# One kernel on one core: the shift columns of the opening on TensorE, the loads of the opening in another order, and three waits of the pair loop moved

## The chip, the core and the metric

One NeuronCore of a Trainium2 chip runs the whole program. The metric is device time in microseconds (us), the median of several executions. Engines are called TensorE (PE in the rows, PEld its weight loads), VectorE (DVE), ScalarE (ACT), GpSimd (POOL) and SyncE (SP, which issues most DMAs).

## What is computed

Two blocks on x (512 tokens, 1024 features, fp32). The change touches the first one:

```python
mod = jax.nn.silu(c) @ w_ada[layer] + b_ada[layer]
shift, scale, gate = jnp.split(mod[:, None, :], 3, axis=-1)
h = rms_norm(x, norm_g[layer]) * (1.0 + scale) + shift
proj = h @ w_in[layer]           # hq hf hi hz rq rk rv rz ga gb
# oA: HGRN2 over chunks, 8 heads; oB: retention over chunks, 8 heads
uA = head_rms_norm(oA, hg_norm_g[layer]) * silu(hz)
uB = head_rms_norm(oB, ret_norm_g[layer]) * silu(rz)
m = sigmoid(ga) * uA + sigmoid(gb) * uB
x = x + gate * (m @ w_out[layer])
```

Retention's q and k are turned (rotary: the two halves of 32 rows of each head are swapped and combined with cos and sin). The second block (convolution, banded attention, two feed-forward layers) follows.

## The kernel before

Features lie on partitions: KC = 8 chunks of 128 features, T = 512 tokens along the free axis. An fp32 product is made of three faster ones: x is split into xa_hi and xa_lo, each weight chunk into w_hi and w_lo, and `dense` does, for each of 8 k, three matmuls of 512 columns (hi x hi, hi x lo, lo x hi): 24 matmuls a chunk (lines 1379 to 1381). A weight chunk of 512 KB is loaded by SyncE into one of four slots of w_raw, ScalarE makes w_hi (`w_high`, line 495), GpSimd makes w_lo (`w_low`, line 431); `ahead(I, j)` on ScalarE makes the w_high of three chunks later. Each engine works through its own program in order; semaphores join them.

**Opening.** x (two DMAs of 1 MB), the scale and shift columns of w_ada (`ada_w`, 8 DMAs of 1 MB: for chunk c the 128 scale columns and the 128 shift columns) and the first four weight chunks are loaded, interleaved. ScalarE squares x, TensorE sums the squares over partitions with a matrix of ones (`sum_squares`), ScalarE makes rstd. VectorE makes silu(c) on all partitions (`c_wide`) and, in `modulation(c)` (lines 908 to 914), two reductions of 1024 elements, one for the scale column and one for the shift column, and the gain column `mix_gain`. `scaled_input(c)` (923) is x * gain * rstd, ScalarE adds the shift column in place (548) and copies to xa_hi (549), GpSimd makes xa_lo for chunks 0 to 5 (438), VectorE for 6 and 7 (929). TensorE computes the first three weight chunks k by k as xa arrives, then chunk 3, and goes into `pair(0)`.

**Pair loop.** Four times (two heads of each kind): 20 weight chunks. The order on TensorE is written out by hand: chunks 0 to 3, `dense_tokens(4)` (values, 96 matmuls of 256 columns, lines 1408 to 1410), 6 and 7 (rotary q and k), `hgrn_levels(0)`, `dense_tokens(10)`, `hgrn_rest(0)`, 12, `ret_scores(0)`, `(1)`, 13, `ret_scores(2)`, `(3)`, `attend(0, 0)`, 14 and so on to 19. The forget gates come from chunks 0 and 1 (ScalarE's sigmoid, line 596, VectorE 1055 to 1059, ScalarE's Ln 603, VectorE's scans and exponents, ScalarE's Exp 567, VectorE's `decayed`, 982 to 996). After that ScalarE copies the values out (616), and for chunks 6 and 7 copies the PSUM bank to `rqk` (623) and, turned, in four pieces of 32 rows to `unit` (626); then comes `ahead(at(7 + n), ...)`, the w_high of chunks 10 and 11. VectorE masks the scores (`near_levels`, `near_eye` line 1018, `causal` 1028 to 1032) out of the four banks of `aps`; a bank is free again when its `taken` semaphore counts up, and TensorE's `attend` waits for that.

## Time and profile before

| | us |
|---|---|
| median of 3 runs | 1752.26 (1751.93 to 1752.62) |
| the profiled execution | 1750.22 |
| its span in the trace | 1748.4 |
| TensorE busy in it | 1671.2 |
| VectorE, ScalarE, GpSimd busy | 809.3, 766.7, 672.1 |

Times in the rows are us from the start of the span. A row of the timeline is: start, duration, engine, line and instruction, what it writes and reads, how many instructions are merged in it, and in brackets how long the engine had idled before it and what ended that. An instruction that waits for the memory port after it has started shows a longer duration.

### The profile page before, as it was taken

What the parts mean: (1) busy time and instruction counts of PE and PEld (TensorE: products, weight loads), DVE (VectorE), ACT (ScalarE), POOL (GpSimd) and SP (SyncE); (2) the same over time, 40 slices, a digit from 0 to 9 for tenths busy, and PEclk for the clock granted to TensorE, in tenths of its full rate; (3) what the DMA queues carried; (4) which work ended last, traced back from release to release, by engine and by line L of the source; (5) the groups of instructions that cost most, each with busy time, mean ns of one, the idle gap of its engine ahead of it and who ended that gap; (6) DMA issues with size and microseconds to landing.
All of it is one profiled execution on the core that took longest, in us unless ns stands there. A gap on an engine that the chain in (4) does not pass through costs nothing.

```text
span 1748.4 us, 22097 instructions
## 1 busy us (share of the span) xinstructions
PE 1671.2 (96%) x8005; PEld 1360.0 (78%) x8005; DVE 809.3 (46%) x1391; ACT 766.7 (44%) x1179; POOL 672.1 (38%) x281
## 2 busy tenths in 40 slices
PE   4899999999999999998999999999999999999997
PEld 2777877877877778875888888888887888888885
DVE  6864564564565539994322122126465321121123
ACT  4544554553553664646443222226476442222222
POOL 3343343343343434312444444445223444344342
PEclk7999999999999999998999999999999999999999
DMA  9321331331331446201223223223211333222231
GB/s 373 103 91 57 103 105 60 101 102 50 107 98 58 134 70 183 96 1 44 90 95 103 89 96 101 92 96 120 73 49 60 98 96 96 96 96 96 96 96 61
DMA packets 49876, 167.59 MB, mean 96 GB/s; under 512 B 4987, under 2 KB 9500, under 8 KB 49308
## 3 DMA queue, kind: packets, MB, share of 16 engines
q1 hardware_dynamic: 43696, 154.50, 26.6%
q10 hardware_dynamic: 6124, 12.33, 3.0%
q8 instruction: 38, 0.62, 0.2%
q14 instruction: 18, 0.15, 0.0%
HBM read 161.56 MB, written 5.24 MB: 95 GB/s over the span
## 4 chain that ended last, share of the span: by engine, by line
PE 83%; DVE 8%; ACT 4%; issue 3%; POOL 1%; DMA 0%; ACTq 0%; DVEq 0%; POOLq 0%
PE gps L1379 23%; PE gps L1381 23%; PE gps L1380 22%; POOL w_lo L431 1%; DVE ada_w L910 1%; PE gps L1408 1%; PE gps L1630 1%; PE gps L1632 1%; PE gps L1631 1%; PE gps L1409 1%; PE gps L1410 1%; PE aps L1548 1%; PE aps L1682 1%; DVE at_near L1005 1%; DVE gates L1125 1%
## 5 line engine op out<-in xcount | busy, mean ns | idle before, releaser
L431 POOL TENSOR_TENSOR w_lo<-w_raw,w_hi 128x1024 fp32r<-128x1024 f32 x260 | 644.8, 2483 | 980.6 <-ACT w_hi L495 980.6
L1379 PE MATMUL gps<-xa_hi,w_hi 128*128 128x512 f32 x1152 | 460.3, 400 | 21.2 <-POOL xa_lo L438 13.3
L1381 PE MATMUL gps<-xa_hi,w_lo 128*128 128x512 f32 x1152 | 450.5, 391 | 0.0
L1380 PE MATMUL gps<-xa_lo,w_hi 128*128 128x512 f32 x1152 | 450.3, 391 | 0.0
L495 ACT CAST w_hi<-w_raw 128x1024 fp32r<-128x1024 f32 x260 | 270.9, 1045 | 154.4 <-PE gps L1381 137.0
L1379 PE MATMUL gps<-xb_hi,w_hi 128*128 128x512 f32 x736 | 291.6, 396 | 2.4 <-issue 1.2
L1381 PE MATMUL gps<-xb_hi,w_lo 128*128 128x512 f32 x736 | 288.9, 393 | 0.0
L1380 PE MATMUL gps<-xb_lo,w_hi 128*128 128x512 f32 x736 | 286.3, 389 | 0.0
L1379 PEld LDWEIGHTS gps<-xa_hi,w_hi 128*128 128x128 f32 x1152 | 217.5, 189 | 74.9 <-issue 18.5
L1380 PEld LDWEIGHTS gps<-xa_lo,w_hi 128*128 128x128 f32 x1152 | 217.7, 189 | 46.2 <-issue 3.1
L1381 PEld LDWEIGHTS gps<-xa_hi,w_lo 128*128 128x128 f32 x1152 | 217.3, 189 | 46.0
L1379 PEld LDWEIGHTS gps<-xb_hi,w_hi 128*128 128x128 f32 x736 | 138.4, 188 | 33.0 <-issue 3.6
L1381 PEld LDWEIGHTS gps<-xb_hi,w_lo 128*128 128x128 f32 x736 | 138.2, 188 | 32.0
L1380 PEld LDWEIGHTS gps<-xb_lo,w_hi 128*128 128x128 f32 x736 | 138.2, 188 | 31.1 <-issue 0.5
L1284 DVE TENSOR_TENSOR hbuf<-gps,rstd 128x512 f32<-128x512 f32 x44 | 30.4, 692 | 202.1 <-PE gps L1381 202.1
L1227 DVE SCALAR_TENSOR_TENSOR aps<-glu,vec,aps 128x512 f32<-128x512 f32 x145 | 99.6, 756 | 1.0
L1408 PE MATMUL gps<-w_hi,xa_hi 128*128 128x256 f32 x256 | 75.4, 295 | 14.5 <-POOL w_lo L431 14.5
L1296 DVE TENSOR_TENSOR res<-gps,res 128x512 f32 x32 | 22.1, 692 | 143.8 <-PE gps L1381 143.8
L1283 DVE TENSOR_TENSOR sq<-gps,rstd 128x512 f32<-128x512 f32 x44 | 30.4, 692 | 121.4 <-PE gps L1381 106.2
L782 ACT ACTIVATE sq<-sq 128x512 f32<-128x512 f32 x44 | 27.9, 634 | 118.4 <-DVE sq L1283 118.4
L1409 PE MATMUL gps<-w_hi,xa_lo 128*128 128x256 f32 x256 | 74.9, 293 | 0.0
L1410 PE MATMUL gps<-w_lo,xa_hi 128*128 128x256 f32 x256 | 74.8, 292 | 0.0
(252 smaller groups left out, 1955.0 us busy)
## 6 DMA issues: line engine op xcount, KB each, us to landing
w_raw<-weights_dram SPq DMA_DIRECT2D x268, 512.0 KB, 3.3
ada_w<-ada_in_dram SPq DMA_DIRECT2D x8, 1024.0 KB, 15.8
gates<-ret_tab_dram ACTq DMA_DIRECT2D x4, 1024.0 KB, 5.8
rel_scratch_dram<-rel_rows ACTq DMA_DIRECT2D x1, 3072.0 KB, 34.5
x<-x_turned_dram SPq DMA_DIRECT2D x2, 1024.0 KB, 9.7
res<-xT_dram ACTq DMA_DIRECT2D x1, 2048.0 KB, 8.8
bias<-rel_scratch_dram ACTq DMA_DIRECT2D x1, 2048.0 KB, 8.5
outT_dram<-y SPq DMA_DIRECT2D x8, 256.0 KB, 2.2
```

The costliest lines, as they stand in the source:

```text
L431: TT(w_lo[:, j, :], w_raw[:, j, :], w_hi[:, j, :].bitcast(F32), ALU.subtract).then_inc(lo_ready[j], 1)
L495: nc.scalar.copy(w_hi[:, j, :], w_raw[:, j, :]).then_inc(hi_ready[j], 1)
L782: nc.scalar.activation(sq[:, m, :], sq[:, m, :], ACT.Silu).then_inc(silu_ready, 1)
L1227: made_at[c] = own.mark(STT(bank, src, w, bank, ALU.mult, ALU.add))
L1283: TT(sq[:, m, :], full(I, 2 * m), rstd[:], ALU.mult).then_inc(evicted[2 * m], 1)
L1284: TT(h, full(I, 2 * m + 1), rstd[:], ALU.mult).then_inc(evicted[2 * m + 1], 1)
L1379: mm(gps[:, j, :], w_hi[:, j, w], x[0][:, k, :], start=k == 0, stop=False)
L1380: mm(gps[:, j, :], w_hi[:, j, w], x[1][:, k, :], start=False, stop=False)
L1381: last = mm(gps[:, j, :], w_lo[:, j, w], x[0][:, k, :], start=False, stop=k == blocks - 1)
L1408: mm(out, x[0][:, k, tok], wh, start=k == 0, stop=False)
L1409: mm(out, x[1][:, k, tok], wh, start=False, stop=False)
L1410: last = mm(out, x[0][:, k, tok], wl, start=False, stop=k == KC - 1)
```

## The change

- `modulation(c)` on VectorE now only makes the scale column. The shift column is made by TensorE: `shift(c)` is 8 fp32 matmuls, the 128 x 128 pieces of w_ada (laid out for it by the host) as weights and one column of silu(c), repeated 128 times, as moving operand, into a bank of `aps` or `gps`; ScalarE adds b_ada to the first column of the result.
- ScalarE makes xa_hi from `hbuf` and the shift column in one instruction instead of two; VectorE makes all xa_lo, from the unshifted `hbuf`; GpSimd makes no xa_lo in the opening.
- silu(c) as a column (`c_col`) is made in two small instructions; `vec` is loaded before `c_wide`.
- Both halves of x are loaded first; w_raw 0, 1, 2 behind ada chunks 2, 4, 6; ScalarE's w_high of chunks 1 and 2 at c = 3 and 6.
- TensorE does five shift blocks before the first dense part and the others between dense parts, whose order is new.
- In the pair loop: `ahead` stands before the copies of chunks 6 and 7, the bank is given back after the first copy, and the turned copies read `rqk` instead of the bank; `near_eye(1)` stands before `take_norm(0, 1)` and `z_gate(17)`; chunk 13 is cut at k = 6, and `ret_scores(2)` and `(3)` stand in the cut.

```diff
-XB_PAD = 240
+XB_PAD = 224
+        c_col = sb("c_col", [P, 2, KC], where=first)
+        shift_at = [aps[:, 1, 0:P], aps[:, 2, 0:P], aps[:, 3, 0:P], gps[:, 3, 0:P]]
@@ SyncE
+            for c in range(2):
+                k = slice(c * KC // 2, (c + 1) * KC // 2)
+                sp.dma_start(x0[:, k, :], x_turned.rearrange("(k p) t -> p k t", p=P)[:, k, :]).then_inc(x_in[c], 16)
             for c in range(KC):
-                if c < 2:
-                    k = slice(c * KC // 2, (c + 1) * KC // 2)
-                    sp.dma_start(x0[:, k, :], x_turned.rearrange("(k p) t -> p k t", p=P)[:, k, :]).then_inc(x_in[c], 16)
                 sp.dma_start(ada_w[:, 2 * c:2 * c + 2, :], ada_in[2 * c:2 * c + 2].rearrange("c p k -> p c k"))\
                   .then_inc(ada_loaded[c], 16)
-                if 2 <= c < 5:
-                    load(0, c - 2)
+                if c in (2, 4, 6):
+                    load(0, c // 2 - 1)
@@ GpSimd
-            for c in range(KC - LAST_LOW):
-                if c < 3:
-                    w_low(0, c)
-                pool.wait_ge(xh_ready, c + 1)
-                TT(xa_lo[:, c, :], hbuf[:, c % 4, :], xa_hi[:, c, :].bitcast(F32), ALU.subtract).then_inc(x_ready, 1)
+            for c in range(3):
+                w_low(0, c)
@@ ScalarE
+            act.dma_start(vec[:], vec_in).then_inc(vec_loaded, 16)
             act.dma_start(c_wide[:, 0, :], c_in.to_broadcast([P, D])).then_inc(c_loaded, 16)
-            act.dma_start(vec[:], vec_in).then_inc(vec_loaded, 16)
+            act.wait_ge(vec_loaded, 16)
+            nc.scalar.activation(c_col[:, 1, :], vec[:, VEC["c"]:VEC["c"] + KC], ACT.Sigmoid).then_inc(c_sig, 1)
...
-                if c == KC // 2 - 1:
+                if c == 1:
                     act.wait_ge(c_loaded, 16)
...
-                if c < 3:
-                    w_high(0, c)
+                if c in (0, 3, 6):
+                    w_high(0, c // 3)
+                act.wait_ge(shift_full, c + 1)
+                own.mark(nc.scalar.activation(mod[:, c:c + 1], shift_at[c % len(shift_at)][:, 0:1], ACT.Identity, bias=vcol("b_ada", c)))
                 act.wait_ge(h_ready, c + 1)
-                own.done(nc.scalar.activation(hbuf[:, c % 4, :], hbuf[:, c % 4, :], ACT.Identity, bias=mod[:, c:c + 1]))
-                nc.scalar.copy(xa_hi[:, c, :], hbuf[:, c % 4, :]).then_inc(xh_ready, 1)
+                own.wait()
+                nc.scalar.activation(xa_hi[:, c, :], hbuf[:, c % 4, :], ACT.Identity, bias=mod[:, c:c + 1]).then_inc(xh_ready, 1)
...
-                    nc.scalar.copy(rqk[:, n, :], b)
+                    ahead(at(7 + n), (7 + n) % SLOTS)
+                    nc.scalar.copy(rqk[:, n, :], b).then_inc(evicted[2 + n], 1)
+                    act.wait_ge(evicted[2 + n], at(6 + n) + 2)
                     for r in range(0, P, ROT_HALF):
                         o = r ^ ROT_HALF
-                        last = nc.scalar.copy(unit[o:o + ROT_HALF, n, :], b[r:r + ROT_HALF, :])
-                    last.then_inc(evicted[2 + n], 1)
-                    ahead(at(7 + n), (7 + n) % SLOTS)
+                        last = nc.scalar.copy(unit[o:o + ROT_HALF, n, :], rqk[r:r + ROT_HALF, n, :])
+                    last.then_inc(turn_ready, 1)
@@ VectorE
+            dve.wait_ge(c_sig, 1)
+            TT(c_col[:, 0, :], vec[:, VEC["c"]:VEC["c"] + KC], c_col[:, 1, :], ALU.mult).then_inc(c_col_ready, 1)
...
             def modulation(c):
                 dve.wait_ge(ada_loaded[c], 16)
-                for n, col in ((2 * c, KC + c), (2 * c + 1, c)):
-                    own.mark(nc.vector.tensor_tensor_reduce(
-                        ada_w[:, n, :], ada_w[:, n, :], c_wide[:, 0, :], op0=ALU.mult, op1=ALU.add, scale=1.0,
-                        scalar=vcol("b_ada", col), accum_out=mod[:, col:col + 1]))
-                own.wait()
+                col = KC + c
+                own.done(nc.vector.tensor_tensor_reduce(
+                    ada_w[:, 2 * c, :], ada_w[:, 2 * c, :], c_wide[:, 0, :], op0=ALU.mult, op1=ALU.add, scale=1.0,
+                    scalar=vcol("b_ada", col), accum_out=mod[:, col:col + 1]))
...
+                STT(xa_lo[:, c, :], hbuf[:, c % 4, :], mod[:, c:c + 1], xa_hi[:, c, :].bitcast(F32), ALU.add, ALU.subtract)\
+                    .then_inc(x_ready, 1)
+
+            gain_at = {c: modulation(c) for c in range(3)}
+            for c in range(3):
+                scaled_input(c)
             for c in range(KC):
-                modulation(c)
-
-                if c >= 2:
-                    for n in range(0, 3) if c == 2 else (c,):
-                        scaled_input(n)
-            for c in range(KC - LAST_LOW, KC):
+                if c + 3 < KC:
+                    gain_at[c + 3] = modulation(c + 3)
                 input_low(c)
+                if c + 3 < KC:
+                    scaled_input(c + 3)
...
-                    was_evicted(6 + n)
+                    dve.wait_ge(turn_ready, p * 2 + (n + 1))
...
                 was_evicted(16)
+                near_eye(1)
                 take_norm(0, 1)
                 z_gate(17, 1, 1, "ret_norm_g")
-                near_eye(1)
                 branch_gate(18, 0, 1)
@@ TensorE
-            for k in range(KC - 3):
+            def shift(c):
+
+                pe.wait_ge(ada_loaded[c], 16)
+                if c >= len(shift_at):
+                    pe.wait_ge(xh_ready, c - len(shift_at) + 1)
+                for k in range(KC):
+                    last = mm(shift_at[c % len(shift_at)], ada_w[:, 2 * c + 1, k * P:(k + 1) * P], c_col[:, 0, k:k + 1].to_broadcast([P, P]),
+                              start=k == 0, stop=k == KC - 1)
+                last.then_inc(shift_full, 1)
+
+            def opening(c, k0, k1):
+                dense(START["pairs"], c, xa, operand=x_wait(X_MIX) if c == 0 else None, part=(k0, k1))
+
+            pe.wait_ge(c_col_ready, 1)
+            for c in range(5):
+                shift(c)
+            opening(0, 0, 3)
+            shift(5)
+            opening(0, 3, 4)
+            shift(6)
+            opening(1, 0, 4)
+            shift(7)
+            for c in range(2):
+                opening(c, 4, 6)
+            opening(2, 0, 6)
+            for k in range(6, KC):
                 for c in range(3):
-                    dense(START["pairs"], c, xa, operand=x_wait(X_MIX) if c == 0 else None, part=(k, k + 1))
-            for c in range(3):
-                dense(START["pairs"], c, xa, operand=x_wait(X_MIX) if c == 0 else None, part=(KC - 3, KC))
+                    opening(c, k, k + 1)
...
-                feature(13)
+                feature(13, 0, 6)
                 ret_scores(2)
                 ret_scores(3)
+                feature(13, 6)
                 attend(0, 0)
```

## Rows read from the trace of the kernel before

**Rows 1.** The page, busy time, share and instructions of each engine.
```profile
PE 1671.2 (96%) x8005; PEld 1360.0 (78%) x8005; DVE 809.3 (46%) x1391; ACT 766.7 (44%) x1179; POOL 672.1 (38%) x281
```

**Rows 2.** Waits of TensorE, whole span: us in total, times, longest.
```profile
PE gps L1408 <- POOL w_lo L431: 14.5, 4, 3.6
...
PE aps L1548 <- DVE at_near L1018: 3.1, 3, 1.1
PE aps L1536 <- DVE at_r L1032: 2.4, 4, 0.6
```

**Rows 3.** Windows: busy of each engine, granted clock, DMA share, GB/s.
```profile
20.00:30.00 10.00, 0.00 (x0) 0.00 (x0) 9.81 (x14) 6.24 (x10) 4.47 (x2) 0.57 1.03 421
90.00:100.00 10.00, 6.38 (x43) 6.05 (x42) 8.88 (x18) 5.93 (x8) 8.06 (x3) 0.83 0.27 92
160.00:170.00 10.00, 8.80 (x46) 6.82 (x45) 2.62 (x4) 3.49 (x6) 0.09 (x1) 1.00 0.00 0
```

**Rows 4.** Timeline of the opening: the sums of squares, rstd, the first w_lo.
```profile
9.19 10.08 PE L1417 MATMUL aps<-sq,ones 128*128 128x512 f32 x16 [9.19 <-ACT sq L514]
...
21.41 0.63 ACT L520 ACTIVATE rstd<-lnv 128x512 f32<-128x512 f32 x1
...
23.16 2.67 POOL L431 TENSOR_TENSOR w_lo<-w_raw,w_hi 128x1024 fp32r<-128x1024 f32 x1 [22.71 <-ACT w_hi L495]
```

**Rows 5.** Timeline of VectorE, end of the opening.
```profile
52.91 1.28 DVE L910 CUSTOM_DVE_ANT_0 ada_w<-ada_w,c_wide,vec 128x1024 f32<-128x1024 f32 x1
...
54.50 0.75 DVE L923 SCALAR_TENSOR_TENSOR hbuf<-x,mix_gain,rstd 128x512 f32<-128x512 f32 x1
55.17 0.69 DVE L929 TENSOR_TENSOR xa_lo<-hbuf,xa_hi 128x512 fp32r<-128x512 f32 x1
```

**Rows 6.** Timeline from the first sigmoid of the pairs to the Ln.
```profile
60.33 0.60 ACT L596 ACTIVATE forget<-gps 128x512 f32<-128x512 f32 x1
...
61.94 7.76 POOL L431 TENSOR_TENSOR w_lo<-w_raw,w_hi 128x1024 fp32r<-128x1024 f32 x3 [0.44 <-ACT w_hi L495]
...
67.48 2.77 DVE L1059 TENSOR_SCALAR forget<-forget 128x1024 f32<-128x1024 f32 x1
...
70.60 1.06 ACT L603 ACTIVATE forget<-forget 128x1024 f32<-128x1024 f32 x1
```

**Rows 7.** Timeline of the first pair, before dense_tokens(10).
```profile
87.60 2.36 ACT L626 COPY unit<-gps 32x512 f32<-32x512 f32 x4
...
91.12 3.38 POOL L431 TENSOR_TENSOR w_lo<-w_raw,w_hi 128x1024 fp32r<-128x1024 f32 x1 [15.96 <-ACT w_hi L495]
...
95.21 4.68 POOL L431 TENSOR_TENSOR w_lo<-w_raw,w_hi 128x1024 fp32r<-128x1024 f32 x2 [0.71 <-ACT w_hi L495]
...
97.83 0.55 PE L1408 MATMUL gps<-w_hi,xa_hi 128*128 128x256 f32 x1 [3.62 <-POOL w_lo L431]
```

**Rows 8.** Timeline of TensorE: dense matmuls of the opening, then hgrn_levels(0).
```profile
37.70 0.80 PE L1379 MATMUL gps<-xa_hi,w_hi 128*128 128x512 f32 x1 [2.34 <-POOL w_lo L431]
...
41.28 0.63 PE L1381 MATMUL gps<-xa_hi,w_lo 128*128 128x512 f32 x1
41.70 0.52 PE L1379 MATMUL gps<-xa_hi,w_hi 128*128 128x512 f32 x1
...
44.12 0.39 PE L1380 MATMUL gps<-xa_lo,w_hi 128*128 128x512 f32 x1
44.35 0.39 PE L1381 MATMUL gps<-xa_hi,w_lo 128*128 128x512 f32 x1
...
90.92 3.29 PE L1476 MATMUL aps<-packed 128*128 128x128 f32 x28
```

**Rows 9.** Timeline of GpSimd, first pair, during decayed(1).
```profile
132.59 5.08 POOL L431 TENSOR_TENSOR w_lo<-w_raw,w_hi 128x1024 fp32r<-128x1024 f32 x1 [5.57 <-ACT w_hi L495]
```

**Rows 10.** Timeline, first pair, hgrn_rest(1) and near_eye(1).
```profile
159.63 1.06 PE L1486 MATMUL aps<-q,key 128*128 128x128 f32 x8
...
162.26 0.71 DVE L1018 COPY_PREDICATED at_near<-eye_mask,aps 128x512 f32<-128x512 int32 x1
```

More of the change, by code:

```diff
@@ L288, in program @@
         prep_done = sem("prep_done")
+        turn_ready = sem("turn_ready")
         rot_ready = sem("rot_ready")
@@ L921, in scaled_input @@
                     dve.wait_ge(x_ready, c - 3)
-                own.wait()
+                own.wait(gain_at[c])
                 STT(hbuf[:, c % 4, :], x0[:, c, :], mix_gain[:, c:c + 1], rstd[:], ALU.mult, ALU.mult).then_inc(h_ready, 1)
@@ L1453, in at, with feature @@
                     return p * (PAIR_CHUNKS // SLOTS) + (START["pairs"] + c // SLOTS)
-                def feature(c):
-                    dense(at(c), c % SLOTS, xa)
+                def feature(c, k0=0, k1=KC):
+                    dense(at(c), c % SLOTS, xa, part=(k0, k1))
                 def bank(u):
@@ L1817, in ada_chunks @@
 def ada_chunks(w_ada):
-    order = [n for c in range(KC) for n in (KC + c, c)]
-    return np.stack([np.ascontiguousarray(w_ada[:, c * P:(c + 1) * P].T) for c in order])
+    return np.stack([m for c in range(KC) for m in (np.ascontiguousarray(w_ada[:, (KC + c) * P:(KC + c + 1) * P].T),
+                                                    chunk(w_ada[:, c * P:(c + 1) * P]))])
 def token_order():
```

9 lines of the change are left out of this document (5 added, 4 removed).

## The prediction

> **What bounds the kernel now.** I read the page first: TensorE is busy 1671.2 us of a 1748.4 us span [rows 1], so a change can win little more than TensorE's gaps and its slow-clock time. The list of waits of TensorE says where the gaps are: beside the opening, three places inside the pair loop, each met once in each of four pairs: 14.5 us in four waits of dense_tokens(10) for w_lo, 3.1 us in three waits for near_eye(1) before attend(1,1) (the fourth is booked as "issue"), and 2.4 us in four waits of attend(0,0) for the causal masks [rows 2]. The windows view shows one such place whole, 1.20 us idle in 160 to 170, and the clock: 0.83 in 90 to 100, around the first w_lo wait [rows 3]. In the opening, rstd is ready at 22.04, but VectorE then still has half of the modulation to do, and GpSimd's subtractions take turns with it; the last low part xa_lo(7) comes after the one that starts at 55.17 [rows 4, 5]. After that the way to the first scans runs over the sigmoid of chunk 0 at 60.33, three w_lo of GpSimd that end at 69.70, the max on VectorE (67.48 to 70.25) between them, and the Ln at 70.60 [rows 6]. TensorE is then ahead of that chain, which comes to it again as the w_lo wait at 97.83 [rows 7]. So a microsecond won at the Ln is won at 97.83, and from there TensorE sets the pace.
>
> **Opening: what VectorE and GpSimd lose.** VectorE gives up 8 of 16 reductions and takes over six xa_lo from GpSimd, which keeps three w_lo here. Unit prices [rows 5]: a reduction with its gain column 1.48 us (52.91 to 54.50 without the 0.11 that the next instruction waits for it), a scaled input 0.67, a low part 0.67; a w_lo that shuts VectorE out 2.35 (2.67 less the 0.3 that it itself waited at 23.16, rows 4). The reductions 0 to 2 are done before 22.04, as the first five are today. From 22.04 to the end of xa_lo(2): 5 scaled inputs (3.4), 3 reductions (4.4), 3 low parts (2.0), 2 w_lo (4.7), 14.5 us, so 36.6. xa_lo(0) comes at about 29. The rest of VectorE's opening (2 reductions, 3 scaled inputs, 5 low parts, one w_lo) could end by 48.
>
> **Opening: what TensorE takes on.** A shift column block is 8 fp32 matmuls of 128 columns. The nearest row is hgrn_levels: 28 records of that form, two to a matmul, start to end 3.2 us, 0.113 each [rows 8]; so 16 records, 1.8 us a block, 3.6 at the lower clock. The moving operand there is a real tile, here one column repeated; no row shows that. Bounds: 1.8 (same form), and twice that. I take 1.8, the row of the same size. Blocks 0 to 4 run from 19.3, where the sums end [rows 4], to about 28.5, beside the wait for rstd and the first low part: they cost nothing; that cover gone they would cost 9 us. Blocks 5 to 7 stand between parts of the opening's dense work and count. From xa_lo(2) to the end of chunk 0, TensorE does 60 matmuls of 512 columns at 0.227 us (44.12 to 44.35) and 3 blocks: 13.6 + 5.4 = 19.0 us. It has been mostly idle from 29 to 36.6; today such a stretch leaves it at half speed (41.28 to 41.70, 0.42 a matmul) until some 4 us after work resumed at 37.70 [rows 8]. That is 2.0 us lost. Chunk 0 is full at 36.6 + 19.0 + 2.0 + 0.4 drain = 58.0, and VectorE, with everything by 50, is no longer what it waits for. Today ScalarE starts the sigmoid of chunk 0 at 60.33, so this is 2.2 us earlier: the three w_lo, which follow that sigmoid, the max and the Ln move with it, Ln at 68.4. Chunk 3 is full at 58.0 + 30 matmuls (6.8) = 64.8; with its sigmoid and a table load it is ready at 66.7, before the max. Gain 2.2 us. With no slow clock it is 4.2, with blocks at the double price -3.2.
>
> **Opening: the rest.** ScalarE swaps an add and a copy per chunk for a one-column bias and one activation; it waits for block c first, and behind it are queued w_high(0,1) and w_high(0,2). Last in line is block 7 (ends about 48.2), bias, high part, xa_lo(7) about 50.2; TensorE asks for it at about 57, 7 us of cover. Moved loads: x is first on SP's queue, so the first ada chunk comes 1 MB later, 2.5 us at 421 GB/s [rows 3]; but the last one has the same 12.8 MB before it and in it as today, 30 us at that rate and a little more from the start, so it lands near 34, while reduction 7 and block 7 start near 40 and 46. vec goes before c_wide on ScalarE's queue; the sigmoid of c_wide sits in a gap of the square sums. w_raw 1 and 2 are issued behind two more ada chunks and land by about 32, used at 27 (slot 1, landing 26) and 42. Nothing for these. Should slot 1 be late, its 12 matmuls are still needed only at 44.
>
> **Pairs: w_high ahead of the rotation's copies.** ScalarE now does w_high for chunks 10 and 11 before the copies of chunks 6 and 7. The four turning copies take 2.36 us and one rqk copy 0.6, so the second w_high is 3.0 us earlier [rows 7]. The first w_lo asks GpSimd at 88.2 instead of 91.12, but VectorE is then in a run of 18 back-to-back multiplications that ends at 92.3. Today's w_lo at 91.12 took 3.38 for 2.35 of work: it got in only at that end. The same run for the other head gives the stronger row: asked at 132.59, it took 5.08, 2.7 us of it waiting through the multiplications [rows 9], and so in all four pairs. So the first w_lo ends at 94.5 as before; only the second gains, by following at once: it ends at about 97.1 instead of 97.56. I take 0.5 us a pair, 2.0 in all. Bounds: nothing, and the whole 3.0 (12 us). The new wait of ScalarE for its own rqk copy is followed by the turning copies, with w_high 11 queued behind; VectorE wants their result only after near_levels(0). Copies from SBUF instead of PSUM: same size, I take the same time.
>
> Here the Trainium skill says otherwise ("SBUF — State Buffer", section "Who interferes with whom"): whoever issues first has the shared pair for one whole instruction and the other blocks. By that rule the w_lo would enter at the next instruction boundary, a rival below; the 5.08 us row speaks against it.
>
> **Pairs: near_eye(1) forward.** Today it runs 162.26 to 162.97 behind take_norm(0,1) and z_gate(17), which waits for a sigmoid [rows 10]; its input is complete when the 8 records from 159.63 are, near 160.6, and near_levels(1), which stays ahead of it, ends about then, so it will be done at 161.4, before TensorE's last hgrn_rest matmul. The whole gap goes: 1.2 + 3 x 1.03 = 4.3 us [rows 2, 3]. What now waits behind it, z_gate(17), frees a bank that the next pair wants 20 us later. Least gain 0, if near_levels(1) ran late.
>
> **Pairs: feature(13) split.** Six of its 24 matmuls (1.4 us) now stand between ret_scores(3) and attend(0,0), more than the 0.6 us that it waits for masks. 4 x 0.6 = 2.4 us [rows 2]. The banks of ret_scores(2) are freed by the masks of ret_scores(0) and (1), which VectorE makes while feature(13) runs. Chunk 13's sigmoid is 0.9 us later; VectorE is then still masking. Least gain 0.
>
> **Sum.** 2.2 + 2.0 + 4.3 + 2.4 = 10.9 us off the 1748.4 us span; what lies around the span (1750.2 in that execution) stays, and that execution is 0.1% under the median of 1752.3. So 1741.4.
>
> **Clock in the pairs.** Behind the first w_lo wait the clock is low: 0.83 of a 10 us window is 3.4 us at half speed [rows 3], 1.7 us of work lost, and it can fall behind each of the four waits, which are all 3.6 us long. They become 3.1 us, in the first pair about 4.6, as TensorE is further ahead there. I change nothing for it; by that window four such losses are 6.8 us, which it can give back or take.
>
> **Rivals.** (a) GpSimd gets in at an instruction boundary. Then the first w_lo runs 88.4 to 90.8, VectorE's multiplications end 2.35 later, hgrn_levels(0) waits for its second half until 93.5 and ends near 95.8, and dense_tokens(10) starts there: 2.0 us a pair instead of 0.5, TensorE idle under 2 us and the clock stays up: +6 and up to +6.8: 1728.6 to 1735.4, say 1732. Chance 0.15. (b) TensorE pays the double price for the blocks, or the pair waits only change their name: opening -3.2, pairs 8.7: 1746.8; or opening 2.2 and half of the pairs: 1745.7. Chance 0.17. (c) The change does not do what it says: the order is TensorE's program, so all three pair waits would have to reappear elsewhere and the opening stay; 1752.3, or a little less. Chance 0.06. (d) Slower: TensorE stays at half clock from 36.6, because blocks of 128 columns between the dense parts do not bring it up. Then 19.0 us of work take 38, chunk 0 is full at 75, 14.7 us after today's sigmoid; less 8.7 from the pairs, 1758.3. It beats the pairs' gain once 13 us of that work is done slow (4.3 us are today's slack of chunk 0, 8.7 the pairs). Against it: with dense work alone it came up within 4 us, and the fp32 records of rows 8 run at the full rate. Chance 0.04.
>
> **Numbers.** Likeliest 1741.4 with 0.58, its own range 1737 to 1746 (clock, half of each pair term). With (a) and (b) the range is 1732 to 1747.5. A measurement tells 0.2%, 3.5 us, from no change: faster 0.89, same 0.07, slower 0.04.
>
> **What would show it.** xa_lo(2) near 36.6, the sigmoid of chunk 0 near 58, the Ln near 68.4; block records of 0.11 us at full clock; no wait of TensorE for near_eye or for masks; the first w_lo of each pair about 6 us long with its wait, and dense_tokens(10) still waiting 3 us. The prediction fails if blocks 5 to 7 hold up xa_lo(5) to (7), if that w_lo is short, or if the clock digits of the pairs change.

## The result, and the profile after

| | before | after |
|---|---|---|
| median | 1752.11 us (1751.93 to 1752.62) | 1727.41 us (1726.04 to 1728.03) |
| ratio after to before | | 0.9858, 95% interval 0.984 to 0.9875 |
| profiled execution, and its span | 1750.2 and 1748.4 us | 1726.04 and 1724.2 us |

The kernel is 24.7 us faster; 10.9 were predicted, and 1727.41 lies below the range. The sign was right and the size was not. The rest of this document is about the 14 us that the prediction did not have. Every trace is one execution: that of the kernel after is the fastest of its four (1726.04), and that of the kernel before lies 1.9 us under its median.

Engines of the kernel after, from the page, to be held against [rows 1]:

```profile
PE 1674.9 (97%) x8133; PEld 1370.3 (79%) x8133; DVE 816.2 (47%) x1382; ACT 763.5 (44%) x1180; POOL 674.8 (39%) x275
```

TensorE has 128 records more (the shift columns) and its span is 24.2 us shorter: all of the gain came out of its gaps and out of the length of its matmuls.

Waits of TensorE of the kernel after, whole span (us in total, times, longest), to be held against [rows 2]:

```profile
PE gps L1418 <- POOL w_lo L436: 6.3, 4, 3.3
...
PE gps L1389 <- DVE xa_lo L937: 5.1, 2, 3.3
PE aps L1509 <- DVE packed L995: 3.9, 7, 0.7
```

The wait for w_lo fell from 14.5 to 6.3 us, those for near_eye and for the causal masks are no longer in the list, and one is new: hgrn_levels (the scans that TensorE does on VectorE's `packed`) waits for VectorE's multiplications, 3.9 us in seven places.

Windows of the kernel after (busy of each engine, granted clock, DMA share, GB/s), the same three as in [rows 3]:

```profile
20.00:30.00 10.00, 7.76 (x63) 7.04 (x62) 9.90 (x14) 6.24 (x13) 4.64 (x2) 1.00 1.02 409
90.00:100.00 10.00, 7.41 (x62) 7.44 (x63) 8.91 (x10) 1.73 (x3) 4.68 (x3) 1.00 0.48 159
160.00:170.00 10.00, 10.00 (x42) 7.56 (x41) 3.95 (x4) 6.49 (x9) 4.93 (x2) 1.00 0.27 79
```

The first shows the shift columns in a stretch in which TensorE had done nothing, the second the clock at full speed (1.00, was 0.83) around the first w_lo wait, the third the gap of near_eye closed.

Timeline of the opening, kernel after:

```profile
7.50 1.15 ACT L516 ACTIVATE sq<-x 128x512 f32<-128x512 f32 x2 [2.97 <-DMA x<-x_turned_dram]
...
17.58 5.52 PE L1460 MATMUL aps<-c_col,ada_w 128*128 128x128 f32 x48
...
19.87 0.63 ACT L522 ACTIVATE rstd<-lnv 128x512 f32<-128x512 f32 x1
...
33.48 0.74 DVE L937 SCALAR_TENSOR_TENSOR xa_lo<-hbuf,mod,xa_hi 128x512 fp32r<-128x512 f32 x1
...
35.73 3.62 PE L1460 MATMUL aps<-c_col,ada_w 128*128 128x128 f32 x16
40.10 1.95 PE L1460 MATMUL aps<-c_col,ada_w 128*128 128x128 f32 x16
...
47.74 0.75 DVE L937 SCALAR_TENSOR_TENSOR xa_lo<-hbuf,mod,xa_hi 128x512 fp32r<-128x512 f32 x1 [3.33 <-ACT xa_hi L555]
...
56.18 0.60 ACT L602 ACTIVATE forget<-gps 128x512 f32<-128x512 f32 x1 [4.81 <-PE gps L1391]
...
57.80 7.76 POOL L436 TENSOR_TENSOR w_lo<-w_raw,w_hi 128x1024 fp32r<-128x1024 f32 x3 [5.26 <-ACT w_hi L497]
...
66.14 1.06 ACT L609 ACTIVATE forget<-forget 128x1024 f32<-128x1024 f32 x1 [1.26 <-DVE forget L1069]
```

The row at 33.48 is xa_lo(2), done at about 34.2. rstd ends at 20.50 (22.04 in [rows 4]), three shift blocks take 5.52 us at the full clock and one takes 3.62 at half of it, the sigmoid of chunk 0 starts at 56.18 and the Ln at 66.14 (60.33 and 70.60 in [rows 6]).

Where the 24.2 us of span are, from the starts of three instructions in both traces. The Ln of the first pair comes 4.5 us earlier (70.60 to 66.14). From there to the first matmul of w_out, behind the four pairs, it is 507.7 us before (to 578.26) and 491.2 us after (to 557.38): 16.4. From there to the end it is 1170.1 and 1166.8: 3.3, in stages in which not one instruction was changed. These 3.3 are net of the clock: in this part the trace of after has 25.7 us at the lower granted clock and that of before 16.8.

### The profile page after: what moved, and what is told of

Read it like the earlier page. It is cut to its first block, busy times and chain, and to the rows that moved or that the text cites. A ratio compares the mean times of both kernels' runs of the same rounds, so it can differ in the third digit from the quotient of the medians.

```text
span 1724.2 us, 22350 instructions
## 1 busy us (share of the span) xinstructions
PE 1674.9 (97%) x8133; PEld 1370.3 (79%) x8133; DVE 816.2 (47%) x1382; ACT 763.5 (44%) x1180; POOL 674.8 (39%) x275
## 4 chain that ended last, share of the span: by engine, by line
PE 89%; DVE 4%; ACT 3%; issue 2%; POOL 2%; DMA 0%; ACTq 0%; DVEq 0%; POOLq 0%
PE gps L1389 24%; PE gps L1391 24%; PE gps L1390 24%; POOL w_lo L436 2%; PE gps L1418 1%; PE gps L1420 1%; PE gps L1419 1%; PE gps L1664 1%; PE gps L1666 1%; PE gps L1665 1%; PE aps L1581 1%; PE aps L1427 1%; PE aps L1716 1%; PE aps L1509 1%; PE aps L1587 1%
## 5 line engine op out<-in xcount | busy, mean ns | idle before, releaser
L436 POOL TENSOR_TENSOR w_lo<-w_raw,w_hi 128x1024 fp32r<-128x1024 f32 x260 | 659.4, 2540 | 960.9 <-ACT w_hi L497 960.8
```

The lines of the kernel that those rows point to most:

```text
L436: TT(w_lo[:, j, :], w_raw[:, j, :], w_hi[:, j, :].bitcast(F32), ALU.subtract).then_inc(lo_ready[j], 1)
```

## Experiments

All ratios are to the kernel before on the same chip. A distance "above the kernel after" is one of medians from two chips; by the ratios it comes out up to 2 us larger (6.8 instead of 5.2 us in experiment 1), and each ratio is known to about 0.0016, which is 3 us. "Half" is a stretch of TensorE at 1.2 instead of 2.4 GHz by the granted clock of the records. A "pair" is the distance from VectorE's first multiplication in decayed(0) to that of the next pair.

**1. The last part undone: XB_PAD back to 240.**

```diff
-XB_PAD = 224
+XB_PAD = 240
```

> The changed kernel with XB_PAD back at 240, nothing else. From the convolution's end on, the changed kernel gained another 3.0 us although no instruction there was changed; its 512-column matmuls follow each other at 226.7 ns on average, those of before at 228.2. Theory A: the place of xb_hi, xb_lo and what lies behind them sets this; then the matmuls of the feed-forward stages are back near 228 ns and the time is 3 to 5 us above the changed kernel's 1727.4, near 1731. Theory B: the pace comes from something else of the build (the new instructions, where the code lies); then nothing changes, 1727 to 1728.

Measured: 1732.59 us median, ratio 0.9897 (0.988 to 0.9913), 5.2 us above the kernel after (0.9858). The size of one unused array, which the prediction had not costed, is worth about a fifth of the change by the medians.

**2. That part alone, in the kernel before.**

```diff
-XB_PAD = 240
+XB_PAD = 224
```

> The kernel before with XB_PAD 224 alone. Theory A (the place of xb sets the matmul pace): 3 to 5 us faster than before, 1747 to 1749, with the opening and the pairs as they were. Theory B: no change, 1752.

Measured: 1747.64 us, ratio 0.9977 (0.9967 to 0.9988): 2.9 us by the medians, 4.0 by the ratio. It acts without any of the other edits.

**3. Pad and opening only** (rotation, near_eye and feature(13) as before; the lines of the rotation are those of experiment 4).

```diff
-                near_eye(1)
                 take_norm(0, 1)
                 z_gate(17, 1, 1, "ret_norm_g")
+                near_eye(1)
...
-                feature(13, 0, 6)
+                feature(13)
                 ret_scores(2)
                 ret_scores(3)
-                feature(13, 6)
...
```

> The changed opening and XB_PAD 224 with the pair loop of before. Theory of the traces: the Ln of the first pair comes at 66.1 (4.5 us earlier than before), the pairs keep their three waits of 3.6, 1.1 and 0.6 us and mostly their slow clock behind the longest (up to 6.8 us), the later stages gain what the pad gives (3 to 4 us): 1743 to 1745. Rival: the pair loop has gained because the opening moved its phase, not by its own edits; then the time is below 1738.

Measured: 1742.25 us, ratio 0.9944 (0.9927 to 0.996), 5.4 us below experiment 2; Ln at 65.92. Its list of TensorE's waits has the three entries of [rows 2] again:

```profile
PE gps L1417 <- POOL w_lo L436: 14.8, 4, 4.0
...
PE aps L1580 <- DVE at_near L1027: 3.1, 3, 1.0
PE aps L1568 <- DVE at_r L1041: 2.4, 4, 0.6
```

**4. All but the rotation.**

```diff
-                    ahead(at(7 + n), (7 + n) % SLOTS)
-                    nc.scalar.copy(rqk[:, n, :], b).then_inc(evicted[2 + n], 1)
-                    act.wait_ge(evicted[2 + n], at(6 + n) + 2)
+                    nc.scalar.copy(rqk[:, n, :], b)
                     for r in range(0, P, ROT_HALF):
                         o = r ^ ROT_HALF
-                        last = nc.scalar.copy(unit[o:o + ROT_HALF, n, :], rqk[r:r + ROT_HALF, n, :])
-                    last.then_inc(turn_ready, 1)
+                        last = nc.scalar.copy(unit[o:o + ROT_HALF, n, :], b[r:r + ROT_HALF, :])
+                    last.then_inc(evicted[2 + n], 1)
+                    ahead(at(7 + n), (7 + n) % SLOTS)
...
-                    dve.wait_ge(turn_ready, p * 2 + (n + 1))
+                    was_evicted(6 + n)
```

> The changed kernel with the copies of chunks 6 and 7 and the place of their w_high as before; near_eye(1) and the cut of chunk 13 stay. Theory: the w_lo wait of dense_tokens(10) is 3.6 us in each pair again, 1.4 us more in three pairs, and the slow clock comes back behind some of them (1.7 us of work each time it does, up to 6.8): 1731 to 1739. Rival: the clock stays up because the other two waits are gone, and only 4 to 5 us are lost: 1731 to 1732.

Measured: 1735.09 us, ratio 0.9905 (0.9889 to 0.9922): the rotation is worth 7.7 us, where 2.0 had been forecast; near_eye and feature(13) together are worth 7.2 (experiment 3 to this). The timeline of its first pair:

```profile
81.60 2.52 DVE L991 TENSOR_TENSOR packed<-packed,q 128x256 f32<-128x256 f32 x7 [0.99 <-ACT hbuf L575]
...
86.42 3.40 POOL L436 TENSOR_TENSOR w_lo<-w_raw,w_hi 128x1024 fp32r<-128x1024 f32 x1 [15.92 <-ACT w_hi L497]
...
90.45 4.69 POOL L436 TENSOR_TENSOR w_lo<-w_raw,w_hi 128x1024 fp32r<-128x1024 f32 x2 [0.63 <-ACT w_hi L497]
...
93.06 0.55 PE L1417 MATMUL gps<-w_hi,xa_hi 128*128 128x256 f32 x1 [3.97 <-POOL w_lo L436]
```

and the window of 90 to 100 us, with the clock at 0.83:

```profile
90.00:100.00 10.00, 6.95 (x46) 6.98 (x47) 8.34 (x15) 1.32 (x2) 4.69 (x2) 0.83 0.49 160
```

dense_tokens(10) starts 11.46 us behind the first multiplication (11.53 in the other pairs). In the kernel after it is 10.77 in the first pair and 10.68 in the others, so 0.7 to 0.85 us of the 7.7 / 4 = 1.9 us per pair are idle time saved. The other part goes with the clock: this kernel has a half stretch in each pair (3.4, 6.8, 3.4 and 3.4 us), the kernel after in none.

**5. near_eye(1) back behind z_gate(17).**

```diff
-                near_eye(1)
                 take_norm(0, 1)
                 z_gate(17, 1, 1, "ret_norm_g")
+                near_eye(1)
```

> The changed kernel with near_eye(1) back behind take_norm(0,1) and z_gate(17). Theory of the traces: TensorE waits 1.0 to 1.2 us before attend(1,1) in each pair again, nothing else moves: 4.2 us more than the changed kernel, 1731.6. Rival: the wait is partly paid back at the next w_lo wait of the pair after, because VectorE and ScalarE are then further ahead: 1728 to 1730.

Measured: 1732.67 us, ratio 0.9896 (0.9879 to 0.9912), 5.3 above the kernel after. The trace has no half stretch in the pairs, as that of after, so it gives the idle time alone: a pair takes 129.5 us instead of 128.2, 1.3 us, 5.2 in four. The wait of 3.1 us in three places is back.

**6. feature(13) whole.**

```diff
-                feature(13, 0, 6)
+                feature(13)
                 ret_scores(2)
                 ret_scores(3)
-                feature(13, 6)
```

> The changed kernel with chunk 13 in one piece. In pairs 1 to 2, where the clock was full in both kernels, the period shrank by 2.72 us while the idle rows lost 3.03; 0.3 us a pair are missing. Theory: the cut itself costs them (other small matmuls between dense ones), so undoing it costs 0.6 less 0.3, 4 times: 1728.6. Rival: the cut gives its full 0.6 and the 0.3 is lost elsewhere: 1729.8.

Measured: 1728.98 us, ratio 0.9872 (0.9856 to 0.9889), 1.6 above the kernel after; the wait of 2.4 us in four places is back, and its two pairs without a half stretch take 128.86 and 128.97 us, 0.7 more than after's. So 1.6 to 2.8 us, with 2.4 forecast; the ratio alone would not tell it from the kernel after, the trace of the wait does.

**7. The second half of x back behind the first ada chunk.**

```diff
-            for c in range(2):
-                k = slice(c * KC // 2, (c + 1) * KC // 2)
-                sp.dma_start(x0[:, k, :], ...).then_inc(x_in[c], 16)
             for c in range(KC):
+                if c < 2:
+                    k = slice(c * KC // 2, (c + 1) * KC // 2)
+                    sp.dma_start(x0[:, k, :], ...).then_inc(x_in[c], 16)
```

> The changed kernel with the second half of x loaded behind the first ada chunk as before (vec stays ahead of c_wide). In the changed kernel the first half of x landed 0.9 us earlier and rstd came 1.5 us earlier than before. Theory A: the order of the x loads gives this; then rstd is near 22.0, the Ln 1.5 us later, 1728.9. Theory B: the order of vec and c_wide gives it (the small vec first, c_wide not in the way of x), or the phase of the clock; then the first square starts at 7.5 still, and the time is unchanged, 1727.4.

Measured: 1727.63 us, ratio 0.987 (0.9854 to 0.9887), not to be told from the kernel after. The first square stays early (7.32), the fifth waits 1.23 us for x, rstd ends at 21.14 and the Ln starts at 65.64. Neither of the last two can be told from the kernel after: in the twelve traces with its opening unchanged (after itself and experiments 1, 3 to 6, 8 to 11, 13 and 14) rstd ends between 19.79 and 21.43 and the Ln starts between 65.34 and 67.51. Single traces of one opening differ by 2 us at the Ln.

**8. XB_PAD 256.** 224 and 256 are 128 bytes apart and 240 is in the middle; the theory was that a multiple of 128 bytes counts.

```diff
-XB_PAD = 224
+XB_PAD = 256
```

> The changed kernel with XB_PAD 256. With 224 the 512-column matmuls of the feed-forward stages follow each other at 226.7 ns in four kernels, with 240 at 228.2 in two. 240 puts xb_hi, xb_lo and all behind them 64 bytes off a multiple of 128 bytes from where 224 and 256 lie. Theory A: the alignment to 128 bytes counts: 226.7 again and 1727.4. Theory B: the distance to something else counts (which rows lie under which), 224 is merely a lucky place: 228 and 1731.

Measured: 1741.26 us, ratio 0.9941 (0.9925 to 0.9958), 13.9 above the kernel after. The 128-byte theory fell: 256 is worse than 240.

**9. A gap for GpSimd between VectorE's two times seven multiplications.**

```diff
-PAIR_STEPS = 27
+PAIR_STEPS = 29
...
-                        TT(q_part, q_part, right(qe, level), ALU.mult)
+                        ins = TT(q_part, q_part, right(qe, level), ALU.mult)
+                    own.done(ins)
```

> The kernel after, with VectorE waiting for its own seven in-place multiplications before the seven copies of the scan's preparation, so that its run of back-to-back instructions has a gap of one completion. Theory A (a GpSimd instruction asked for in mid-run is held until VectorE's next gap): in pair 0 the first w_lo of the three starts doing work near 84.5 instead of 87.7, its group of three goes from 11.0 to about 7.5 us each, PE's wait of 3.29 for w_lo falls under 1, the pair is 2 to 3 us shorter; in the pairs where it already got in (about 0.99 left) VectorE's extra gap costs at most 0.2 us on a path with slack: in all 1 to 3 us, 1724.5 to 1726.5. Theory B (the gap is of no use, because the request is held by something else than the run of instructions): 3.29 stays, and the time is 1727 to 1728.

Measured: 1737.86 us, ratio 0.9922 (0.9905 to 0.9939), 10.5 above the kernel after; both theories missed. First pair:

```profile
83.35 2.50 POOL L436 TENSOR_TENSOR w_lo<-w_raw,w_hi 128x1024 fp32r<-128x1024 f32 x1 [12.97 <-ACT w_hi L497]
...
87.05 1.16 PE L1510 MATMUL aps<-packed 128*128 128x128 f32 x8 [1.73 <-DVE packed L996]
...
87.44 2.43 POOL L436 TENSOR_TENSOR w_lo<-w_raw,w_hi 128x1024 fp32r<-128x1024 f32 x1 [1.59 <-ACT w_hi L497]
...
90.93 4.64 PE L1510 MATMUL aps<-packed 128*128 128x128 f32 x20 [2.73 <-DVE packed L996]
```

and its window of 90 to 100 us:

```profile
90.00:100.00 10.00, 9.07 (x53) 9.07 (x54) 8.34 (x20) 1.42 (x2) 2.37 (x1) 0.66 0.34 105
```

GpSimd now gets in twice (2.50 and 2.43 us, hardly any waiting), the second time ahead of the multiplications that TensorE waits for. The wait of dense_tokens(10) for w_lo is gone from TensorE's list, and the one for packed has grown:

```profile
PE aps L1510 <- DVE packed L996: 14.9, 8, 2.7
```

It was 3.9 us in seven places in the kernel after: the wait changed its name and grew by 4.7 us net (14.9 against 3.9 + 6.3). The clock followed: half stretches of 6.8, 3.4, 6.8 and 3.4 us, one in each pair, the first of them the 0.66 of that window. The pairs take 132.1, 130.8 and 132.1 us.

**10 and 11. XB_PAD 352 and 480**, 512 and 1,024 bytes behind 224.

> The kernel after with the unused array in front of xb_hi 352 wide instead of 224: what follows it lies 512 bytes further along each partition. Theory A (what counts is where the 512-column row blocks stand against a multiple of 512 bytes): the matmuls of 512 columns keep 226.7 ns start to start from 600 on, and the time stays 1726 to 1729. Theory B (against a multiple of 2,048 bytes, which is the length of such a block): the cadence is longer, 228 to 232 ns, and the time 1732 to 1742. Theory C (against no multiple at all, the distance itself costs, as 224, 240 and 256 gave 226.7, 228.2 and 229 to 232): above 232 ns and over 1745.

> The same with 480: 1,024 bytes further. Theory A (512 bytes): 226.7 ns, 1726 to 1729. Theory B (2,048 bytes): 228 to 232 ns, 1732 to 1742. If 352 is slow and this one is not, the unit is 1,024 bytes. Theory C: over 1745.

Measured: 1727.55 us, ratio 0.9859 (0.9843 to 0.9876), and 1727.1 us, ratio 0.9861 (0.9845 to 0.9877). Both are the kernel after. So it is neither the distance nor a multiple of 2,048 bytes: 224, 352 and 480, all equal up to a multiple of 512 bytes, give one time, and 240 and 256 do not. The groups by line, 800 to 1000 us, in the order before (240), after (224), 256, 352 (out<-in, count, busy us, mean ns):

```profile
L1379 PE MATMUL gps<-xb_hi,w_hi 128*128 128x512 f32 x154 | 61.1, 397 | 0.0
L1379 PE MATMUL gps<-xa_hi,w_hi 128*128 128x512 f32 x120 | 46.7, 389 | 0.0
```

```profile
L1389 PE MATMUL gps<-xb_hi,w_hi 128*128 128x512 f32 x185 | 72.4, 391 | 0.0
L1389 PE MATMUL gps<-xa_hi,w_hi 128*128 128x512 f32 x107 | 41.6, 389 | 0.0
```

```profile
L1389 PE MATMUL gps<-xb_hi,w_hi 128*128 128x512 f32 x175 | 69.5, 397 | 0.0
L1389 PE MATMUL gps<-xa_hi,w_hi 128*128 128x512 f32 x113 | 44.0, 389 | 0.0
```

```profile
L1389 PE MATMUL gps<-xb_hi,w_hi 128*128 128x512 f32 x182 | 71.2, 391 | 0.0
L1389 PE MATMUL gps<-xa_hi,w_hi 128*128 128x512 f32 x111 | 43.2, 389 | 0.0
```

Of these rows only those that move xb change, 397 ns against 391; those that move xa, which lies ahead of the array, are 389 everywhere. The length does not tell 240 from 256, so it is no measure of the price. What sets the pace is the distance of starts. Fourteen in a row, kernel after and then XB_PAD 256 (first and last of each):

```profile
899.66 0.39 PE L1389 MATMUL gps<-xb_hi,w_hi 128*128 128x512 f32 x1
...
902.61 0.39 PE L1390 MATMUL gps<-xb_lo,w_hi 128*128 128x512 f32 x1
```

```profile
899.68 0.39 PE L1389 MATMUL gps<-xb_hi,w_hi 128*128 128x512 f32 x1
...
902.71 0.39 PE L1390 MATMUL gps<-xb_lo,w_hi 128*128 128x512 f32 x1
```

That is 2.95 / 13 = 0.2269 and 3.03 / 13 = 0.2331 us, and in the kernel before 2.98 / 13 = 0.2292. There are 736 x 3 = 2208 such matmuls: 2208 x 6.2 ns = 13.7 us for 256 (13.9 measured), 2208 x 2.3 ns = 5.1 us for 240 (5.2 and 2.9 to 4.0 measured). The whole traces say the same: behind one another at full clock, the matmuls that move xb start every 226.8 to 226.9 ns in all thirteen traces with 224, 352 or 480, every 229.0 and 229.2 in the two with 240 and every 232.9 with 256, and those that move xa every 227.1 to 227.3 in all sixteen. From the first matmul of w_out to the end it is 1164.8 to 1167.1 us in the thirteen, 1170.1 and 1170.2 with 240 and 1180.1 with 256. What the runs do not separate is the place of xb by itself from its distance to arrays that did not move, such as the weights that the same matmuls load.

**12. vec and c_wide asked for in the old order.**

```diff
-            act.dma_start(vec[:], vec_in).then_inc(vec_loaded, 16)
             act.dma_start(c_wide[:, 0, :], c_in.to_broadcast([P, D])).then_inc(c_loaded, 16)
+            act.dma_start(vec[:], vec_in).then_inc(vec_loaded, 16)
```

> The kernel after with ScalarE's first two DMAs in the order of before (c_wide, then vec). Theory A (the earlier first square, 8.42 to 7.50, comes from vec being asked for first): the first square goes back to about 8.4, the first three w_lo and Ln of pair 0 come 0.9 later, 1728 to 1729. Theory B (it comes from elsewhere, the second half of x or the starting time of the DMAs): first square at 7.3 to 7.6, and the time is unchanged, 1726 to 1728.5.

Measured: 1729.56 us, ratio 0.9879 (0.9862 to 0.9895), with a wide spread (1726.83 to 1732.4); the interval overlaps that of the kernel after. The first square is back at 8.36 and the first half of x lands at 8.33, as in the two traces with the old order (8.33 and 8.40); with vec first it lands at 7.30 to 7.65 in all thirteen. So these 0.9 us do come from the order of the two loads. rstd ends at 22.23, 1.7 us later than in the trace of after, of which the squares' start explains 0.9; the Ln starts at 66.80, inside the spread of unchanged openings. Of the 2.2 us between the medians no more than that is shown to be in the opening: this trace has three half stretches in the pairs.

**13 and 14. GpSimd's request made 0.1 and 0.3 us later.** In the first, one such copy stands, in the second three, into different columns.

```diff
+                    if n == 0:
+                        nc.scalar.copy(r_col[:, 0, 0:1], eps_col[:])
                     ahead(at(7 + n), (7 + n) % SLOTS)
```

> The kernel after with one 128x1 copy of ScalarE in front of the w_high whose w_lo GpSimd asks for during VectorE's run of 14 multiplications (once a pair): the request comes 0.1 to 0.2 us later. So far, in the traces of the kernels with the change at the rotation, the request fell 155 to 172 ns behind the start of a VectorE instruction and 30 of 40 got in (took 2.5 us); requests at 258 to 396 ns and at 46 to 85 ns never did. Theory A (the position inside the instruction decides): at about 270 to 370 ns the request is held to the end of the run in all four pairs (first w_lo about 6.2 us), TensorE waits some 3.3 us for w_lo in each, and where the clock falls behind it the pair takes 129.8 instead of 128.2 us: in all 1728 to 1734. Theory B (it is chance, whatever the position): one to four of the four get in, 1726 to 1729.

> The same with three such copies, the request 0.3 to 0.6 us later. Theory A: where it falls near 160 ns behind the start of a VectorE instruction again it gets in in most pairs, 1726 to 1729; elsewhere in none, 1728 to 1734. Theory B: as before, some get in whatever the position. Theory C (clock): whatever happens to w_lo, each pair without a half-clock stretch takes 128.2 to 128.5 us and each with one of 3.4 us takes 129.7 to 130.0, so the median goes by the number of such pairs.

Measured: 1728.18 us, ratio 0.9871 (0.9854 to 0.9887), and 1733.27 us, ratio 0.9899 (0.9883 to 0.9916). With one copy the request came 252 to 262 ns behind the start of VectorE's sixth multiplication; it was held in the first pair and got in in the other three. Theory A's premise, that requests at 258 to 396 ns never get in, is wrong: one at 262 did, and the one that was held came at 252. With three copies it came about 100 ns behind the start of the seventh, and was held in all four. Second pair of the kernel after, where it gets in, and of the kernel with three copies, where it is held:

```profile
210.17 4.72 DVE L992 TENSOR_TENSOR packed<-packed,q 128x256 f32<-128x256 f32 x7 [1.01 <-ACT hbuf L575]
...
212.02 2.51 POOL L436 TENSOR_TENSOR w_lo<-w_raw,w_hi 128x1024 fp32r<-128x1024 f32 x1 [12.97 <-ACT w_hi L497]
...
215.70 1.15 PE L1509 MATMUL aps<-packed 128*128 128x128 f32 x8 [0.73 <-DVE packed L995]
216.21 6.72 POOL L436 TENSOR_TENSOR w_lo<-w_raw,w_hi 128x1024 fp32r<-128x1024 f32 x2 [1.68 <-ACT w_hi L497]
...
220.85 0.36 PE L1418 MATMUL gps<-w_hi,xa_hi 128*128 128x256 f32 x1 [0.99 <-POOL w_lo L436]
```

```profile
211.06 2.51 DVE L996 TENSOR_TENSOR packed<-packed,q 128x256 f32<-128x256 f32 x7 [1.01 <-ACT hbuf L575]
...
213.19 10.71 POOL L436 TENSOR_TENSOR w_lo<-w_raw,w_hi 128x1024 fp32r<-128x1024 f32 x3 [13.23 <-ACT w_hi L497]
...
221.84 0.50 PE L1422 MATMUL gps<-w_hi,xa_hi 128*128 128x256 f32 x1 [2.85 <-POOL w_lo L436]
```

Where it gets in, the seven multiplications take 4.72 instead of 2.51 us, and the second w_lo is asked for at 216.21, in the middle of what is left of VectorE's run, and is held in its turn (6.72 us for two, where two in a row without VectorE in the way take 4.69, as at 90.45 in experiment 4). dense_tokens(10) starts 10.68 us behind the first multiplication in the one case and 10.78 in the other. Getting in early gains 0.1 us.

The window around that wait, three copies and then the kernel after:

```profile
215.00:225.00 10.00, 7.15 (x47) 6.85 (x46) 9.71 (x12) 6.17 (x9) 8.90 (x3) 0.84 0.32 105
```

```profile
215.00:225.00 10.00, 7.80 (x63) 7.46 (x63) 9.56 (x17) 5.04 (x7) 6.72 (x2) 1.00 0.42 129
```

And the pairs of both as windows. With three copies the first pair has no half stretch, the next two have one each:

```profile
82.76:211.06 128.30, 124.76 (x677) 104.64 (x677) 79.92 (x140) 65.32 (x82) 52.44 (x18) 1.00 0.28 91
211.06:340.84 129.78, 126.93 (x682) 106.87 (x681) 79.88 (x140) 65.21 (x82) 50.83 (x18) 0.99 0.28 89
340.84:470.64 129.80, 126.94 (x682) 106.87 (x681) 79.89 (x140) 65.21 (x82) 50.88 (x18) 0.99 0.27 89
```

```profile
210.17:338.39 128.22, 126.00 (x682) 105.36 (x681) 80.18 (x140) 65.02 (x79) 51.25 (x18) 1.00 0.29 90
```

Held without a half stretch 128.30, not held 128.22, held with a half stretch of 3.4 us 129.8. Theory C is borne out in the traces: the length of a pair goes by the clock. The nine traced kernels that have all the pair edits as in after (after itself and experiments 1, 7, 8 and 10 to 14) show 27 such distances: 17 without a half stretch are 128.18 to 128.35 us, whether GpSimd got in or not; seven with one of 3.4 us behind a held request are 129.66 to 129.82; two first pairs with one where it had got in are 128.54 and 128.60; one with 6.8 us is 130.74.

## Why the prediction was wrong, point by point

| term | forecast | measured |
|---|---|---|
| opening, to the Ln | 2.2 | 4.5 (trace), 5.4 (experiments 2 to 3) |
| near_eye | 4.3 | 5.2 |
| feature(13) | 2.4 | 1.6 to 2.8 |
| rotation, idle time | 2.0 | about 3 (0.7 to 0.85 a pair, experiment 4) |
| clock in the pairs | 0, up to 6.8 | about 5.4 (trace) |
| XB_PAD | not costed | 3 to 5 |

**Opening: mechanism right, size short by 2.3.** Every block cost what was forecast (1.84 for 1.8, 3.62 for 3.6 at half), blocks 0 to 4 were hidden, and the last xa_lo at 47.74 had the cover that it was given. The predicted milestones came early from the first on: xa_lo(2) done at 34.2 instead of 36.6. Of these 2.4 us, 1.5 are rstd, ready at 20.50 and not at 22.04: the step that put "vec goes before c_wide on ScalarE's queue" at nothing failed. Experiment 12 shows 0.9 of the 1.5, the earlier landing of x, to come from that order; the other 0.6 lie in the stage of the squares, whose length differs by more than that between traces of one opening, and stay open. The last 0.9 of the 2.4 are work of VectorE: the two w_lo cost it 2.1 and 2.0 us instead of 4.7 together, and a reduction with its column took 1.40 instead of 1.48. Behind xa_lo(2), 22.0 us passed to the sigmoid where 21.4 were forecast (TensorE stayed at half clock until about 39.6), and from there 10.0 to the Ln, where 10.4 had been taken. How much of an early rstd reaches the Ln the runs do not show: experiments 7 and 12 moved rstd by 0.6 and 1.7 us, and both of their Ln lie within the 2 us by which the Ln differs between unchanged openings. For the same reason the 2.3 us by which this term was short are known to about 1 us.

**near_eye and feature(13): right.** The whole gap of near_eye went, as forecast; it was worth 1.3 us a pair instead of 1.07, 0.2 more than the wait that the list showed. feature(13) gave its 0.6 to 0.7 us a pair.

**Rotation: the idle time 1 us short, and the reason right in part.** The forecast was that the first w_lo stays held to the end of VectorE's run, that only the second gains by following at once, and that this is worth 0.5 us a pair. Where it was held (the first pair of the kernel after, all four of experiment 14) just this happened: dense_tokens(10) starts 10.77 instead of 11.46 us behind the first multiplication in the first pair, 0.7 less, and 10.78 instead of 11.53 in the others. Rival (a) happened as well: in three of the four pairs of the kernel after, GpSimd got in. But what the rival was to bring, 2.0 us a pair and so 1.5 more than a held request, it did not, but 0.1: the second w_lo was held instead (216.21 above), and TensorE lost in hgrn_levels what it won at dense_tokens(10). Rival (a) had the event right and the price wrong. Its time, 1732, was nearer because it counted the clock, and by luck: the 6 us of idle time that it added did not come, and about as much came from the opening and from XB_PAD, which it did not price.

The Trainium skill's page "SBUF — State Buffer", section "Who interferes with whom", says that the one of VectorE and GpSimd that issues first holds the shared ports for its whole instruction and the other is blocked. The prediction took from it that a request gets in at the next boundary between two instructions. Of the requests in these traces some do and most do not (33 of 44 during one instruction of the run, none during five others, below), so that reading does not hold as a rule; which boundary is open the section does not say.

**The clock: the step that failed.** The prediction saw the half stretch behind the first w_lo wait, priced four of them at 6.8 us, and wrote "I change nothing for it", because the waits would still be 3.1 us and more. Pairs of the kernel before as windows, the first of these without a half stretch, the second with one of 3.4 us:

```profile
219.82:350.77 130.95, 125.75 (x682) 105.46 (x681) 75.85 (x140) 64.82 (x79) 47.21 (x18) 1.00 0.27 88
350.77:483.24 132.47, 127.19 (x682) 106.94 (x681) 75.81 (x141) 64.81 (x79) 47.21 (x18) 0.99 0.27 87
```

The one without takes 130.95 us, against 128.2 after, so idle time is 2.7 a pair, 11.0 in four, against the 8.7 forecast; the other 5.4 of the 16.4 are the half stretches, 13.6 us of them before and none after. Not every execution has none: the traces of experiments 10 and 11, which equal the kernel after in time, have one half stretch of 3.4 us each in the pairs, so in the medians the clock may be worth some 1.5 us less than 5.4. What the traces show of TensorE just before the clock fell, by the longest wait at dense_tokens(10) and at the scans in front of it:

| longest wait there | where | pairs with a half stretch |
|---|---|---|
| 3.6 to 4.0 us | rotation as before (kernel before, experiments 2 to 4) | 15 of 16 |
| 2.85 to 3.3 us | rotation as after, request held | 11 of 15 |
| 2.65 to 2.73 us, on packed | experiment 9 | 4 of 4 |
| 1.0 to 1.6 us | rotation as after, GpSimd got in | 2 of 29 |

So the rotation seems to have saved the clock mostly by breaking one wait of 3.6 us into three of 0.5 to 1.6, and this would be what GpSimd's getting in is good for: not the 0.1 us but a fall of the clock avoided, about 1.5 us. Length alone does not decide: of the four held requests with a wait of 3.29 us three led to no fall, of the eleven with 2.86 only one, and in experiment 9 2.65 us were enough. No run changed the length of the wait and nothing else, so this is read from counts and not shown.

**XB_PAD: left out.** The prediction named the diff's first line nowhere. It moves 16 floats of an array that nobody reads, and with them everything behind it. 3.3 us of the span were won in stages that the change does not touch; experiments 1, 2, 8, 10 and 11 tie it to where xb lies, up to a multiple of 512 bytes. The trace of before had held the row: 397 ns for the matmuls that move xb and 389 for those that move xa, two groups side by side with the same shape.

**Rivals (b) to (d)** did not come. Of (b), "the pair waits only change their name" was to be seen in small (3.9 us of waiting for packed) and in full in experiment 9. TensorE did come up from half clock with the blocks of 128 columns between its work (35.73 at half, 40.10 at full), which was the case against (d).

By span: 2.3 us more in the opening, 2.3 more idle time saved in the pairs, 5.4 of clock and 3.3 of place make the 13.3 us between the forecast 10.9 and the 24.2. No version beat the kernel after: 352 and 480 equal it, and the gap loses 10.5 us.

## What to carry to other kernels

When a change shortens a wait in front of TensorE, cost the clock behind it too, as a term with its own likeliest value: here it was 5 us where the idle time of the same edit was 3. Read the diff for edits that move addresses, and compare groups of one shape by operand name: where an operand's matmuls are 2% longer than its twin's, it is worth trying other places for its array. And before giving GpSimd a chance to enter VectorE's run, ask who waits for the end of that run: a w_lo that enters moves its 2.4 us onto them.

## What the runs showed of the hardware

- **Place of the moving operand.** fp32r matmuls of 512 columns that move xb start every 226.9 ns where its rows are at the place of XB_PAD 224, or 512 or 1,024 bytes behind it, every 229.2 ns at 64 bytes behind (kernel before) and every 233.1 ns at 128 bytes behind, in the stretch from 900 us. The 31 taps of the convolution, whose moving operand starts one column further for each tap, show no such step: in the kernel after their matmuls start every 230 to 236 ns on average, whatever the tap, 233.2 over all. So place is not the whole of it. Why it should be so, and whether a place between the multiples other than these two is better or worse, was not tried.
- **Who gets in.** In the eleven traced kernels with the rotation as in after and the request during VectorE's sixth multiplication (1.84 to 1.94 us behind the first; experiment 9 among them), GpSimd got in ahead of the seventh in 33 of 44 pairs, with requests from 156 to 262 ns behind the sixth's start, and was held in 11, with requests from 155 to 252. Requests during the seventh (2.12 us, and 2.38 in the other head's run), the tenth (3.15) and the fourteenth (4.8) of VectorE's run of 18 never got in before the run ended or paused, nor did the second request, during the eleventh or twelfth. Where experiment 9 had put a pause between the two times seven, that second request, now in the fourth or fifth instruction behind the pause, got in in four of four. The counts are sure, the reason is open: no position inside the sixth tells the 33 from the 11.
- **Repeated moving column.** fp32 matmuls with 128 columns that all read one column, as the shift columns do, cost what real tiles cost: 5.52 us for 48 records, 0.115 each, against 3.29 for 28 in [rows 8].
